# The weights' diagonal of an expert slot, built on ScalarE behind its GELU instead of on VectorE

## What is computed

```python
def peer_ffn(h, w_query, sub_keys, u_tab, v_tab):
    ...
    best_s, best_c = lax.top_k(cand_s.reshape(M, H, K * K), K)
    ids = jnp.take_along_axis(cand_i.reshape(M, H, K * K), best_c, axis=-1)
    g = jax.nn.softmax(best_s, axis=-1)
    ...
    def block(args):
        xb, idb, gb = args
        u = jnp.take(u_tab, idb, axis=0)
        v = jnp.take(v_tab, idb, axis=0)
        act = jax.nn.gelu(jnp.einsum('nkd,nd->nk', u, xb).astype(f32)) * gb
        return jnp.einsum('nk,nkd->nd', act.astype(v.dtype), v)
```

## Time and profile before

| | |
|---|---|
| median of 3 runs | 2990.7 us (2988.2 to 2991.11) |
| span of the profiled execution | 2989.7 us |
| TensorE matmul busy | 2666.7 us, 89% |
| VectorE busy | 2159.7 us, 72% |
| ScalarE busy | 637.2 us, 21% |
| GpSimd busy | 990.5 us, 33% |
| moved by DMA | 1182.34 MB, of it 1073.81 MB gathers |

### The profile page before, as it was taken

How to read it: one execution, slowest core, us unless ns; L and a number is a source line. 1 busy time by engine, 2 the same in 40 slices (tenths; PEclk the granted TensorE clock), 3 DMA queues, 4 the chain that set the end, 5 groups by cost and what they waited for, 6 DMA issues and landing times.

```text
span 2989.7 us, 35028 instructions
## 1 busy us (share of the span) xinstructions
PE 2666.7 (89%) x11992; PEld 2186.6 (73%) x11992; DVE 2159.7 (72%) x6678; ACT 637.2 (21%) x1699; POOL 990.5 (33%) x1028
## 2 busy tenths in 40 slices
PE   8999999899998888989998888989999887877787
PEld 6778888678887677877887776868787665555555
DVE  1248858787588978687688778778588777678565
ACT  3231311272113116101111215201211110102001
POOL 0013333333333333333333333333333343333332
PEclk9999999999999999999999999999999999999999
DMA  5369999999999999999999999999999999999998
GB/s 190 103 247 426 413 408 426 426 365 409 415 387 392 386 427 405 425 421 427 426 415 416 414 426 416 413 427 423 427 398 407 409 427 426 426 417 411 427 425 344
DMA packets 166802, 1182.34 MB, mean 395 GB/s; under 512 B 19408, under 2 KB 19936, under 8 KB 24032
## 3 DMA queue, kind: packets, MB, share of 16 engines
q0 software_dynamic: 147456, 1073.81, 86.8%
q1 hardware_dynamic: 19168, 106.31, 9.0%
HBM read 1177.95 MB, written 2.10 MB: 395 GB/s over the span
## 4 chain that ended last, share of the span: by engine, by line
PE 53%; DMA 26%; DVE 11%; issue 8%; ACT 1%; POOL 0%; DVEq 0%; SPq 0%; POOLq 0%; ACTq 0%
PE main_bank L337 35%; DMA main_ring<-in_uv,main_idi 26%; PE main_bank L375 9%; PE main_bank L373 5%; DVE main_diagonal L311 2%; DVE main_ring L297 1%; DVE main_pick L202 1%; PE main_bank L543 1%; DVE main_hid L297 1%; DVE main_idf L209 1%; DVE main_topi L162 1%; DVE main_work L154 1%; DVE main_pick L196 1%; PE main_bank L735 1%; DVE main_topi L156 1%
## 5 line engine op out<-in xcount | busy, mean ns | idle before, releaser
L337 PE MATMUL main_bank<-main_ring,main_diagonal 128*128 128x256 f32 (+1 forms) x8160 | 1989.8, 390 | 294.6 <-DVE main_diagonal L311 294.0
L337 PEld LDWEIGHTS main_bank<-main_ring,main_diagonal 128*128 128x128 f32 x8160 | 1536.7, 193 | 656.4 <-DVE main_diagonal L311 434.4
L297 DVE CUSTOM_DVE_ANT_0 main_ring<-main_ring,main_bank 128x1024 f32<-128x1024 f32 x1024 | 1247.8, 1219 | 619.6 <-DMA main_ring<-in_uv,main_idi 607.0
L280 POOL DMA_INDIRECT main_ring<-in_uv,main_idi x1024 | 990.3, 967 | 1977.8 <-PE main_bank L337 1751.1
L302 ACT ACTIVATE main_act_out<-main_hid 128x1 f32<-128x1 f32 x1024 | 206.5, 203 | 2164.8 <-DVE main_hid L297 2153.5
L311 DVE TENSOR_SCALAR main_diagonal<-main_ident,main_act_out,main_gate 128x128 f32<-128x128 f32 x1024 | 359.2, 351 | 21.0 <-ACT main_act_out L302 13.9
L375 PE MATMUL main_bank<-main_xT,main_w_block 128*128 128x256 f32 x1408 | 358.4, 381 | 1.9 <-ACT main_xT L408 1.9
L375 PEld LDWEIGHTS main_bank<-main_xT,main_w_block 128*128 128x128 f32 x1408 | 268.3, 191 | 38.9 <-ACT main_xT L408 2.3
L375 PE MATMUL main_bank<-main_xT_query,main_w_block 128*128 128x256 f32 x512 | 124.2, 379 | 0.9 <-ACT main_xT_query L408 0.9
L375 PEld LDWEIGHTS main_bank<-main_xT_query,main_w_block 128*128 128x128 f32 x512 | 96.6, 190 | 14.5 <-ACT main_xT_query L408 1.2
L302 ACT ACT_TABLE_LOAD x82 | 105.2, 1283 | 1.4
(11 more groups left out here) (196 smaller groups left out, 1206.7 us busy)
## 6 DMA issues: line engine op xcount, KB each, us to landing
main_w_block<-in_w_query SPq DMA_DIRECT2D x32, 1024.0 KB
main_w_block<-in_w_ab SPq DMA_DIRECT2D x24, 1024.0 KB
main_ring<-in_uv,main_idi POOLq DMA_INDIRECT x1024
main_w_block<-in_w_c_in SPq DMA_DIRECT2D x16, 1024.0 KB
main_w_block<-in_w_out SPq DMA_DIRECT2D x8, 1024.0 KB
main_w_block<-in_w_c_out SPq DMA_DIRECT2D x8, 1024.0 KB
main_att_bias<-in_att_bias SPq DMA_DIRECT2D x16, 256.0 KB
main_keys<-in_keysT SPq DMA_DIRECT2D x2, 1024.0 KB, 12.8
```

What stands on the lines that cost most here:

```text
L280: nc.gpsimd.indirect_dma_start(self.ring[n % self.bufs], None, self.uv[p // NT], bass.IndirectOffsetOnAxis(self.choice.idi[:, p % 2, k:k + ...
L297: self.nc.vector.tensor_tensor_reduce(out=row, in0=row, in1=self.ps[:, 6:8], scale=1.0, scalar=0.0, op0=ALU.mult, op1=ALU.add, accum_out=s ...
L337: last = self.nc.tensor.matmul(self.ps[:, 4 + at // T, at % T:at % T + wide], self.diagonal[:, n % DIAGS], self.ring[n % self.bufs][:, D + ...
```

## The change

ScalarE builds the diagonal, right behind the GELU of the same slot. It first multiplies the column `act_out[:, k]` by the gate in place (a Copy with the gate column as scale, L310 after the change), counts the new semaphore `weighed` and waits for it itself, and then scales the identity by that column (L314). The waits for `gated` and for `v_done` of slot n-3 move to ScalarE with it. The calls on VectorE go away: at slot k, where place(k-1) stood behind dot(k), and the last one behind the loop.

```diff
-    def place(self, dve, p, k):
+    def place(self, act, p, k):
         n = p * HK + k
-        dve.wait_ge(self.gelued, n + 1)
+        act.wait_ge(self.gelued, n + 1)
         if k % (2 * PK) == 0:
-            dve.wait_ge(self.choice.gated, p * self.choice.PAIRS + k // (2 * PK) + 1)
+            act.wait_ge(self.choice.gated, p * self.choice.PAIRS + k // (2 * PK) + 1)
+        weight = self.act_out[:, k:k + 1]
+        self.nc.scalar.activation(weight, weight, ACT.Copy, scale=self.choice.gate[:, p % 2, k:k + 1]).then_inc(self.weighed, 1)
+        act.wait_ge(self.weighed, n + 1)
         if n >= DIAGS:
-            dve.wait_ge(self.v_done, n - DIAGS + 1)
-        self.nc.vector.tensor_scalar(self.diagonal[:, n % DIAGS], self.ident[:], self.act_out[:, k:k + 1],
-                                     self.choice.gate[:, p % 2, k:k + 1], ALU.mult, ALU.mult).then_inc(self.placed, 1)
+            act.wait_ge(self.v_done, n - DIAGS + 1)
+        self.nc.scalar.activation(self.diagonal[:, n % DIAGS], self.ident[:], ACT.Copy, scale=weight).then_inc(self.placed, 1)
...
                     experts.activate(act, p, k)
+                    experts.place(act, p, k)
...
-                    if k:
-                        experts.place(dve, p, k - 1)
-                    elif p:
-                        experts.place(dve, p - 1, HK - 1)
...
-            experts.place(dve, 2 * NT - 1, HK - 1)
```

More of the change, by code:

```diff
@@ L263, in __init__ @@
         self.diagonal = room.sb("diagonal", [P, DIAGS, P])
-        (self.gain_in, self.x_there, self.dotted, self.gelued, self.placed, self.v_done, self.added) = (s.sem(f"e_{x}") for x in (
-             "gain_in", "x_there", "dotted", "gelued", "placed", "v_done", "added"))
+        (self.gain_in, self.x_there, self.dotted, self.gelued, self.placed, self.v_done, self.added, self.weighed) = (s.sem(f"e_{x}") for x in (
+             "gain_in", "x_there", "dotted", "gelued", "placed", "v_done", "added", "weighed"))
         self.half_done, self.half_added = s.sem("e_half_done"), s.sem("e_half_added")
```

## The result

The changed kernel takes 2974.84 us in the median of its runs, the kernel before 2990.9 us in the same comparison; the ratio is 0.9947, 95% interval 0.9931 to 0.9963. One of its four runs took 4188.48 us at a mean granted clock of 0.597 (the others 2972.8 to 2975.99 us at 0.983 to 0.984); it stands in the median and not in the ratio. A second comparison, on another chip together with the last three experiments, gave 2975.42 us and a ratio of 0.9955 (0.9941 to 0.9968). The kernel is 14 to 16 us faster. The profiled span went from 2989.7 to 2974.2 us.

A forecast was written before the change was run, and what follows sets the result against it. Bound: the transfer queue, 427 GB/s at most, 77.6 us lost where not full. 13.5 + 4.6 + 1.5 - 3.4 - 4.0 = 12.2 us gained: span 2977.5, forecast 2978.5 us, own range 2965 to 2986, whole range 2953 to 3000.

The forecast's parts named there:

- Costs on ScalarE: ScalarE, per slot: one-column copy 0.30 us, 128-column copy 0.39 us; busy time rises from 637 to about 1340 us.
- Quiet slot: Slot where nothing else goes on: about 4.6 us from dot product to gather issue, where it was 6.28.
- B: Four stretches with VectorE full (990:1030, 2200:2240, 2280:2360, 2660:2770), losing 22.5 us: 60% regained, 13.5 us.
- The signs named for it: 990:1030 and 2280:2360, by their slots, near 427 GB/s; TensorE's gap at VectorE's long run 4 us or less.
- A: Stretches with TensorE nearly without gaps: 820:940 gains 0; attention, 600:680, loses 0.1 us a slot, 3.4 us.
- C: ScalarE's table-switch stretches 1130:1190 and 1830:1880, losing 7.9 us: a cost of 2 us at each, 4 us.
- D: All other losses, thinly spread, 23.0 us: the 1.7 us head start gives back 20%, 4.6 us.
- the tail: Very end: one TensorE sum of about 1.9 us saved, 0.4 us of longer way added: 1.5 us gained.
- The whole gain: First rival: head start works everywhere, ScalarE catches up after table switches without loss: 38.5 us gained, 2952; chance 0.12.
- the third case: Rival: ScalarE becomes the bound where tables are switched: 10 us slower, 3001; chance 0.19.
- the point that decides: Attention stretch: ScalarE becomes the bound if it needs more than 2.86 us a slot; the forecast's sum was 2.83.

The follow-up runs named there:

- e2: The changed kernel, but ScalarE makes the diagonal of slot k-1 behind the GELU of slot k: VectorE relieved, no head start; 2987.73 us, ratio 0.9991.
- e3: The changed kernel, with VectorE still writing an unread 128x128 tile behind each dot product but the first: head start without relief; 2984.54 us, ratio 0.9986.
- e9: The changed kernel with four diagonals in place of three, the fourth in the iota tile; 2968.61 us, ratio 0.9923.
- e4: The changed kernel without ScalarE's copy that multiplies the column by the gate, and without its semaphore wait; 2966.44 us, ratio 0.9913.
- both cures: The changed kernel with four diagonals, and VectorE making the diagonals in slots 60 to 97 of passes 2 and 4; 2964.59 us, ratio 0.9915.
- e5: The kernel before, with VectorE making the diagonal of slot k-1 ahead of the dot product of slot k; 3008.34 us, ratio 1.0058.

## Why the prediction was right, point by point

The sum was 12.2 us gained, 2978.5 us; measured were 15.5 us of span and 2974.84 us. The sign, the order of size and the mechanism were right. Part of the closeness is luck, since two errors cancel: by slots the change gained 25.4 us (24.4 in the other slots of the table, the rest at the two ends), where the forecast had 13.5 + 4.6 + 1.5 = 19.6, and it lost 9.9 us in the 118 slots, where the forecast had 7.4. By its steps:

- *Costs on ScalarE.* 0.30 and 0.39 us forecast, 0.294 and 0.402 measured; 1340 us busy forecast, 1341.2 measured. The column operand's 93 ns, taken from 1024 columns, held for 1 and 128 columns.
- *Quiet slot.* 4.6 us forecast, 4.55 measured.
- *B.* 13.5 us forecast; the four windows went from 22.5 to 7.2 us, 15.3 gained (about 14 by slots). The signs named for it came in part: 990:1030 and 2280:2360, by their slots, reach 396 and 408 GB/s and not 427. One of the two reasons given, one slot less behind each long run of VectorE, shows at the run at slot 12 of pass 2. TensorE there, after:

```profile
975.78 7.07 PE L339 MATMUL main_bank<-main_ring,main_diagonal 128*128 128x256 f32 x32
988.27 6.62 PE L339 MATMUL main_bank<-main_ring,main_diagonal 128*128 128x256 f32 x16 [5.42 <-ACT main_diagonal L314]
```

  The diagonal of slot 12 comes at 979.84, 0.7 us behind its dot product, and TensorE idles 5.42 us instead of 6.30. The forecast said 4 us or less. It left out that TensorE is behind when the run begins, so the early slot lengthens its work ahead of the gap more than it cuts the gap; GpSimd's longest wait there fell from 9.15 to 8.27 us. The other reason, 0.35 us less per slot on a full engine, was named and not priced; by slots relief alone gives about half of what this stretch gained.
- *A.* For 820:940 the gain was put at 0, "an earlier diagonal only waits longer"; the loss fell from 12.6 to 9.8 us. This step is wrong by 2.8 us, and no experiment was made for it alone. From the dot product of slot 90 of pass 1 to that of slot 1 of pass 2 the kernel before took 122.0 us, relief alone (e2) 121.5, the head start alone (e3) 119.7 and the change 118.2: most of it is the head start. How that helps where TensorE has no gap stays open. In the attention stretch 0.1 us a slot was forecast; slots 132 to 174 took 2.864 us each before and 2.962 after (starts of their dot products). The size is right (4.1 us over these 42 slots, 3.4 forecast over 34) and partly by luck: both the sum of ScalarE's times and the wait for `v_done` were named, and the size was read from the first. e9, e4 and e2 show that it is the second.
- *C.* 4.0 us cost forecast; the two windows went from 7.9 to 12.9 us, 5.0. e4 bears out ScalarE's length as cause. Giving the diagonals back returns only 2 to 3 us; these windows lost 7.9 us before the change too.
- *D and the tail.* 4.6 us forecast for D; 77.6 less the named stretches was 23.0 and is 64.6 - 24.0 - 7.2 - 12.9 = 20.5: 2.5 us, within the 3 us to which the totals are known, so D is not decided by it. The tail gained 0.9 us (last dot product's start to the end: 11.2 and 10.3 us) and not 1.5; the sum left out nothing, it sized the saved TensorE work at 1.9 us, where two slots in a row took 3.72 and one 1.99, and added the longer way at 0.4 where it is 0.8.
- *Rivals.* The whole gain (2952) would have needed C without loss; even with both cures the best kernel takes 2964.59. Of the third case, ScalarE as the bound, the losses do occur, in three stretches, at about 10 us by slots in place of 25; but only in the two decays stretches is ScalarE the bound. In the attention stretch it is not: with four diagonals the slot takes 2.80 us with ScalarE busy for 2.65 of them (75.71 us in 28.6 slots). So ScalarE never reached the 2.86 us a slot that the forecast named as the point that decides, and 4 us were lost there all the same, by the wait.
- *The Trainium skill.* The Trainium skill (ScalarE: Activation LUTs, What ACT_TABLE_LOAD costs) has a drain of about 1.38 us behind each load. The rows at 650.54 and 651.83 show the activation 1.29 us behind the load's start, and with four diagonals ScalarE is 95% busy with one switch per slot in a stretch that is faster than before. The trace does not have the drain. The rule of the Trainium skill (ScalarE: Activation LUTs, Rules for kernel authors) to multiply on VectorE holds for the price (0.35 against 0.70 us a slot). Followed here it would have cost time: with the multiplication on ScalarE the kernel is 0.5% faster.

## What to carry to other kernels

In a ring of buffers count how long a slot is held, and not only how busy the engines are: a step that stands behind the next slot's wait adds that wait to the hold of every slot. Here 1.7 us less holding in a quiet slot was worth more (17 us by slots, 0.51% of the time without ScalarE's losses) than 359 us less work on the engine that did the step (11 us, or 0.26% on top). The hold from the dot product on is not all of it: the kernel of e5 had a shorter one than the change in a quiet slot, and was the slowest of all, because landed rows waited ahead of their dot products. Move such a step to the engine that produces its input, and then look there for the buffers that it writes: with three diagonals that engine's other work was held up in the attention stretch, with four it was not. Where that engine has its own rush, give the step back; that was worth 2 to 3 us in the two decays stretches.

## What was not expected of the hardware

An activation that waits for a semaphore which the activation before it counts starts 0.03 to 0.04 us after that one's end (648.36 to 648.39, 648.68 to 648.72), and the next GELU, which waits for nothing on ScalarE, starts 0.09 us ahead of the diagonal's end (649.03, against 648.72 + 0.40). Three dependent activations cost a slot 0.87 us in a row (648.16 to 649.03). The pauses that were allowed for, 0.12 us, are thus nearly paid back by the overlap.
